# Hybrid attention and RG-LRU layer: column sums shared with TensorE, spread softplus chains, and fp32r for the F term and the gate sums

## The reference

```python
mod = silu(c) @ w_ada + b_ada                    # 4096 -> 3 x 4096
shift, scale, gate_res = split(mod, 3)
h = rms(x) * norm_w * (1 + scale) + shift
q, k, v, z_a, f_logit, x_r, z_r = split(h @ w_in)
log_f = log_sigmoid(f_logit + b_f)               # 16 heads
F = cumsum(log_f)
logit[t, s] = q_t . k_s / sqrt(128) + F_t - F_s  # s <= t
y_a = (softmax(logit) @ v * silu(z_a)) @ w_br_attn
xc = causal_depthwise_conv(x_r)                  # 4 taps
a = exp(-8 * sigmoid(xc @ w_rg_a + b) * softplus(-lru_lambda))
hr = scan(a, sqrt(1 - a*a) * sigmoid(xc @ w_rg_x + b) * xc)
y_r = (hr * silu(z_r)) @ w_br_rnn
g_a, g_r = split(sigmoid(h @ w_gate + b_gate))
x = x + gate_res * ((g_a * y_a + g_r * y_r) @ w_out)
```

## Time and profile before

| | |
|---|---|
| median of 3 runs | 2666.55 us (2666.18 to 2667.52) |
| the profiled execution: its time, its span | 2662.13 us, 2660.3 us |
| mean granted TensorE clock | 0.992 |
| TensorE busy | 2585.8 us, 97% of the span |
| VectorE busy | 1930.0 us, 73% |
| ScalarE busy | 1229.5 us, 46% |
| GpSimd busy | 1.2 us |
| DMA | 698.71 MB, mean 263 GB/s |

### The profile page before, as it was taken

One profiled execution on the slowest core, in us unless ns is written; L12 is line 12 of the kernel. 1 busy time (PEld: TensorE's weight loads), 2 busy tenths in 40 slices (PEclk: granted clock), 3 DMA queues, 4 the chain that ended last, 5 costly groups with the idle time before them and its releaser, 6 DMA issues.

```text
span 2660.3 us, 30834 instructions
## 1 busy us (share of the span) xinstructions
PE 2585.8 (97%) x11618; PEld 2134.1 (80%) x11618; DVE 1930.0 (73%) x1949; ACT 1229.5 (46%) x1428; POOL 1.2 (0%) x9
## 2 busy tenths in 40 slices
PE   2999999999999899999999999999999999999999
PEld 2788888888888788777888888878888888888887
DVE  6889999898887556666666666668787878745454
ACT  4554333333343356544656666654343433433333
POOL 0000000000000000000000000000000000000000
PEclk7999999999999999999999999999999999999999
DMA  9999999999998466444666666679898989667675
GB/s 370 327 335 345 330 353 337 338 355 335 348 338 279 128 193 186 120 127 145 196 199 195 199 191 200 197 252 353 306 355 305 353 305 356 216 208 225 209 225 171
DMA packets 351033, 698.71 MB, mean 263 GB/s; under 512 B 26306, under 2 KB 30628, under 8 KB 350628
## 3 DMA queue, kind: packets, MB, share of 16 engines
q1 hardware_dynamic: 350884, 696.74, 78.4%
HBM read 692.45 MB, written 4.19 MB: 262 GB/s over the span
## 4 chain that ended last, share of the span: by engine, by line
PE 93%; DVE 4%; DMA 1%; ACT 1%; issue 1%; SPq 0%; DVEq 0%; ACTq 0%
PE ps_acc L1027 30%; PE ps_acc L1029 30%; PE ps_acc L1036 30%; DVE acc L685 2%; DMA land<-in_w_gate 1%; PE ps_t L1087 1%; PE ps_t L1086 1%; ACT w_hi L510 1%; DVE w_lo L668 1%; PE ps_c L1054 1%; PE ps_t L1131 1%; DMA ada_first<-in_w_ada 0%; PE ps_t L1123 0%; DVE qn L837 0%; PE ps_t L1140 0%
## 5 line engine op out<-in xcount | busy, mean ns | idle before, releaser
L668 DVE TENSOR_TENSOR w_lo<-land,w_hi 128x1024 fp32r<-128x1024 f32 x896 | 1094.7, 1223 | 625.0 <-ACT w_hi L510 624.0
L510 ACT ACTIVATE w_hi<-land 128x1024 fp32r<-128x1024 f32 x896 | 950.5, 1061 | 1285.6 <-PE ps_acc L1029 1069.8
L1027 PE MATMUL ps_acc<-w_hi,h_hi 128*128 128x512 f32 x3072 | 1208.8, 393 | 6.4 <-issue 4.3
L1029 PE MATMUL ps_acc<-w_hi,h_lo 128*128 128x512 f32 x3072 | 1199.4, 390 | 0.0
L1036 PE MATMUL ps_acc<-w_lo,h_hi 128*128 128x512 f32 x3068 | 822.7, 390 | 8.2 <-DVE w_lo L668 8.2
L1036 PEld LDWEIGHTS ps_acc<-w_lo,h_hi 128*128 128x128 f32 x3068 | 576.6, 188 | 130.4 <-DVE w_lo L668 10.3
L1027 PEld LDWEIGHTS ps_acc<-w_hi,h_hi 128*128 128x128 f32 x3072 | 578.4, 188 | 127.2 <-issue 4.3
L1029 PEld LDWEIGHTS ps_acc<-w_hi,h_lo 128*128 128x128 f32 x3072 | 579.0, 188 | 118.3
L685 DVE SCALAR_TENSOR_TENSOR acc<-ada_ring,cvec,acc 128x1024 f32<-128x1024 f32 x217 | 277.7, 1280 | 3.8 <-DMA ada_ring<-in_w_ada 3.5
L926 DVE SCALAR_TENSOR_TENSOR racc<-res_land,cvec,racc 128x1024 f32<-128x1024 f32 x124 | 158.6, 1279 | 1.0 <-DMA res_land<-in_w_ada 1.0
L780 DVE TENSOR_TENSOR store<-ps_acc,store 128x1024 f32<-128x1024 f32 x89 | 108.6, 1220 | 11.8 <-PE ps_acc L1036 11.5
(11 more groups left out here) (168 smaller groups left out, 1027.4 us busy)
## 6 DMA issues: line engine op xcount, KB each, us to landing
land<-in_w_in SPq DMA_DIRECT2D x384, 512.0 KB, 4.9
land<-in_w_gate SPq DMA_DIRECT2D x256, 512.0 KB, 4.5
ada_ring<-in_w_ada SPq DMA_DIRECT2D x224, 512.0 KB, 5.9
res_land<-in_w_ada SPq DMA_DIRECT2D x128, 512.0 KB, 7.1
land<-in_w_out SPq DMA_DIRECT2D x128, 512.0 KB, 4.5
land<-in_w_br_attn SPq DMA_DIRECT2D x64, 512.0 KB, 4.2
land<-in_w_br_rnn SPq DMA_DIRECT2D x64, 512.0 KB, 5.3
ada_first<-in_w_ada SPq DMA_DIRECT2D x32, 512.0 KB, 11.5
```

The lines of the kernel that those rows point to most:

```text
L510: act.activation(w_hi[:, n % PARTS], land[:, n % LAND], ACT.Copy).then_inc(hi_rdy, 1)
L668: dve.tensor_tensor(w_lo[:, n % PARTS], land[:, n % LAND], w_hi[:, n % PARTS].bitcast(F32), ALU.subtract).then_inc(split_done, 1)
L1027: pe.matmul(ps_acc[:, par, t], l_hi(kk, t), w_hi[:, n % PARTS, kk], start=first and kk == 0, stop=False)
L1029: ins = pe.matmul(ps_acc[:, par, t], l_lo(kk, t), w_hi[:, n % PARTS, kk], start=False, stop=False)
```

## The change

- **First adaLN group.** Even tiles stay on VectorE (in slot 3 of `acc`), odd ones go to TensorE: eight fp32 products a tile, the tile as stationary operand and a column of silu(c) as moving one, added up in ps_c and ps_d (`first_tile`). Behind odd tiles 11 to 25 TensorE turns two pieces of x each. The last tile and the sums are made in two halves, and shift and scale, rounding and low parts follow in two halves. SyncE waits for a slot of an odd tile on a count of TensorE's.
- **Small loads** of parameters go from SyncE's queue to ScalarE's. `bf_col` is loaded once, not twice.
- **Softplus** of lru_lambda runs in the first stage, behind tile 24; its exp on ScalarE stands behind the last `take_xt`. The F chain is cut into nine steps between N_F + 7 and N_F + 20.
- **F_t - F_s** is one fp32r product of 64 rows: F split in a high and a low part, on both sides, put in place once by four DMAs; GpSimd multiplies the left side with a one-hot column for each head, into two buffers. `f_product` runs once, 16 columns wide.
- **Heads.** ScalarE instead of VectorE copies the turned probabilities; the maxima come negated from the reduction; on VectorE the head steps come ahead of `head_pre`. The value step waits for ya_lo of the head before, not of the one before that.
- **RG-LRU**: TensorE turns x_r and z_r straight from `store`, without the copy `xz`.
- **Gates**: racc is split in high and low parts and summed by four fp32r products; RES_AT is 5 + t*5//4 for 2 + t*4//3; the sums come four units later; the bias lands in `res_gate` itself; SyncE's wait for unit_done stands at N_R + 4.
- **Last unit**: all 12 products go by row blocks (six for t = 0, then six for t = 1), not only the last four.

```diff
+def ada_done(a):
+    return a // 2 + 1 if a < ADA_T else ADA_T // 2 + a - ADA_T + 1
...
+RSUM_AT = [N_R + (q + 1) * 2 * (GU + RU) for q in range(CH // 2)]
...
-        RES_AT[N_R + q * 2 * (GU + RU) + 2 + t * 4 // 3] = (q, t)
+        RES_AT[N_R + q * 2 * (GU + RU) + 5 + t * 5 // 4] = (q, t)
...
+            pool.wait_ge(f_rows, 64)
+            pool.wait_ge(f_cols, 1)
+            for h in range(HEADS):
+                if h >= 2:
+                    pool.wait_ge(scored, h - 1)
+                pool.tensor_scalar(f_head[:, h % 2], f_left[:], onehot[:, h:h + 1], None, ALU.mult
+                                   ).then_inc(fh_rdy, 1)
...
+                    if a >= FIRST_SLOTS and a % 2:
+                        sp_.wait_ge(ada_by_pe, (a - FIRST_SLOTS) // 2 + 1)
+                    elif a >= FIRST_SLOTS:
+                        sp_.wait_ge(ada_used, ada_done(a - FIRST_SLOTS))
...
+                if n == N_F + 23:
+                    sp_.wait_ge(f_ones, 2)
+                    sp_.wait_ge(f_low, 3)
+                    sp_.dma_start(f_left[32:48, :], f_hi[:].bitcast(F32)).then_inc(f_rows, 16)
+                    sp_.dma_start(f_left[48:64, :], f_rest[:, 0]).then_inc(f_rows, 16)
+                    sp_.dma_start(f_right_raw[0:16, :], f_rest[:, 2]).then_inc(f_rows, 16)
+                    sp_.dma_start(f_right_raw[16:32, :], f_rest[:, 1]).then_inc(f_rows, 16)
...
+                if n == N_R + 4:
+                    sp_.wait_ge(unit_done, N_R)
                 if n in RES_AT:
                     q, t = RES_AT[n]
                     i = q * RES_TILES + t
-                    if i == 0:
-                        sp_.wait_ge(unit_done, N_R)
...
+            act.wait_ge(sp_in, 1)
+            act.activation(spt[:, 1], spt[:, 0], ACT.Exp, scale=-1.0).then_inc(sp_e, 1)
             hi(0)
-            round_h(0)
+            round_first(0)
             hi(1)
+            round_first(1)
...
+                if step == "probs":
+                    act.wait_ge(pr_t, h + 1)
+                    if h:
+                        act.wait_ge(valued, h)
+                    act.activation(prt[:], ps_p, ACT.Copy).then_inc(prt_rdy, 1)
...
+                if n + 2 in RSUM_AT:
+                    q = RSUM_AT.index(n + 2)
+                    act.wait_ge(res_used, (q + 1) * RES_TILES)
+                    if q:
+                        act.wait_ge(rsum, q)
+                    act.activation(racc_hi[:], racc[:], ACT.Copy).then_inc(racc_h, 1)
...
-            for a in range(ADA_T):
+            for a in range(0, ADA_T, 2):
                 ada(a)
-                if a == 2:
+                if a == 4:
                     dve.wait_ge(ss_rdy, NT)
                     dve.tensor_scalar(mx[:], mx[:], 1.0 / D, EPS, ALU.mult, ALU.add).then_inc(ms_rdy, 1)
-                if a == 5:
                     dve.wait_ge(rt_rdy, 1)
                     dve.reciprocal(rstd[:], mx[:]).then_inc(rstd_rdy, 1)
-            mod_h(0)
-            low_h(0)
+                if a == 24:
+                    softplus()
+            mod_tiles(0, KPG // 2, 1, 0)
+            low_tiles(0, KPG // 2, 1)
+            mod_tiles(KPG // 2, KPG, 2, 1)
+            lo(0)
+            low_tiles(KPG // 2, KPG, 2)
...
+            def f_step(off):
+                part = lambda k: lt[:, k]
+                if off == 7:
+                    dve.wait_ge(bf_in, 16)
+                    dve.wait_ge(f_done, 1)
+                    st.did(dve.tensor_scalar(lt[:, 5], bank4[0:HEADS, 0:SEQ], bf_col[:], None, ALU.add))
                     st.sync()
-                    st.did(dve.memset(t_[ones_at:ones_at + 16, :], 1.0))
-                dve.wait_ge(bf_in, 32)
-                dve.wait_ge(f_done, 2)
-                st.did(dve.tensor_scalar(lt[:, 5], bank4[0:48, 0:SEQ], bf_col[0:48, 0:1], None, ALU.add))
-                st.sync()
-                st.did(dve.scalar_tensor_tensor(lt[:, 0], lt[:, 5], -1.0, lt[:, 5], ALU.mult, ALU.max), lf_in, 1)
-            def f_scan():
-                dve.wait_ge(lf_e, 1)
-                log1p_exp(lambda k: lt[:, k])
-                st.did(dve.tensor_scalar(lt[:, 5], lt[:, 5], 0.0, None, ALU.min))
-                st.sync()
-                st.did(dve.scalar_tensor_tensor(lt[:, 5], lt[:, 2], -2.0, lt[:, 5], ALU.mult, ALU.add))
-                st.did(dve.memset(lt[:, 4], 1.0))
-                st.sync()
-                st.did(dve.tensor_tensor_scan(ff[:], lt[:, 4], lt[:, 5], 0.0, ALU.mult, ALU.add))
-                st.sync()
+                    st.did(dve.scalar_tensor_tensor(lt[:, 0], lt[:, 5], -1.0, lt[:, 5], ALU.mult, ALU.max), lf_in, 1)
+                if off == 10:
+                    dve.wait_ge(lf_e, 1)
+                    log1p_ratio(part)
+                if off == 11:
+                    log1p_square(part)
+                if off == 12:
+                    log1p_terms(part, 6, 5)
+                if off == 13:
+                    log1p_terms(part, 4, 3)
+                if off == 14:
+                    log1p_terms(part, 2, 1)
+                if off == 15:
+                    log1p_end(part)
+                    st.did(dve.tensor_scalar(lt[:, 5], lt[:, 5], 0.0, None, ALU.min))
+                    st.sync()
+                    st.did(dve.scalar_tensor_tensor(lt[:, 5], lt[:, 2], -2.0, lt[:, 5], ALU.mult, ALU.add))
+                if off == 16:
+                    st.did(dve.memset(lt[:, 4], 1.0))
+                    st.sync()
+                    dve.tensor_tensor_scan(ff[:], lt[:, 4], lt[:, 5], 0.0, ALU.mult, ALU.add).then_inc(f_sum, 1)
+                if off == 20:
+                    dve.wait_ge(f_rnd, 1)
+                    dve.tensor_tensor(f_rest[:, 0], ff[:], f_hi[:].bitcast(F32), ALU.subtract).then_inc(f_low, 1)
+                    dve.tensor_tensor(f_rest[:, 1], f_hi[:].bitcast(F32), ff[:], ALU.subtract).then_inc(f_low, 1)
...
-                    dve.tensor_copy(prt[:], ps_p).then_inc(prt_rdy, 1)
...
+            def last_unit_by_rows(par, l_hi, l_lo, n):
+                for t in range(NT):
                     for kk in range(UK):
-                        for t in range(NT):
-                            ins = pe.matmul(ps_acc[:, par, t], l_hi(kk, t), w_lo[:, n % PARTS, kk],
-                                            start=False, stop=last and kk == UK - 1)
+                        pe.matmul(ps_acc[:, par, t], l_hi(kk, t), w_hi[:, n % PARTS, kk], start=False, stop=False)
+                        pe.matmul(ps_acc[:, par, t], l_lo(kk, t), w_hi[:, n % PARTS, kk], start=False, stop=False)
+                    if t == 0:
+                        pe.wait_ge(split_done, n + 1)
+                    for kk in range(UK):
+                        ins = pe.matmul(ps_acc[:, par, t], l_hi(kk, t), w_lo[:, n % PARTS, kk],
+                                        start=False, stop=kk == UK - 1)
...
+            def first_tile(a, kks):
+                pe.wait_ge(ada_first_in[a % FIRST_SLOTS], a // FIRST_SLOTS * 16 + 16)
+                for kk in kks:
+                    for s in range(2):
+                        ins = pe.matmul(first_bank(kk)[:, s * KPG + kk:s * KPG + kk + 1],
+                                        ada_first[:, a % FIRST_SLOTS, s, kk * P:(kk + 1) * P], cvec[:, a:a + 1],
+                                        start=a == 1 and s == 0 and kk % (KPG // 2) == 0, stop=False,
+                                        skip_group_check=True)
+                return ins
+            def first_sums(kks):
+                for kk in kks:
+                    for s in range(2):
+                        ins = pe.matmul(first_bank(kk)[:, s * KPG + kk:s * KPG + kk + 1],
+                                        acc[:, FIRST_ACC, s, kk * P:(kk + 1) * P], ones[:, 0:1], start=False, stop=True,
+                                        skip_group_check=True)
+                ins.then_inc(colsum, 1)
...
-                        pe.matmul(out, fl[:, t * P:(t + 1) * P], fr[:, 0:(t + 1) * P], start=True, stop=False)
+                        pe.matmul(out, f_head[:, h % 2, t * P:(t + 1) * P], f_right[:, 0:(t + 1) * P], start=True,
+                                  stop=False)
...
-                        pe.wait_ge(ya_rdy, h - 1)
+                        pe.wait_ge(ya_rdy, h)
...
+            pe.wait_ge(silu_c, 1)
+            for a in range(1, ADA_T - 1, 2):
+                first_tile(a, range(KPG)).then_inc(ada_by_pe, 1)
+                if 11 <= a < 27:
+                    for i in range(a - 11, a - 9):
+                        turn_x(i)
+            halves = range(KPG // 2), range(KPG // 2, KPG)
+            first_tile(ADA_T - 1, halves[0])
+            pe.wait_ge(ada_used, ada_done(ADA_T - 2))
+            first_sums(halves[0])
+            first_tile(ADA_T - 1, halves[1])
+            first_sums(halves[1])
...
+                    for i, bank in enumerate((ps_c, ps_d)):
+                        pe.matmul(bank[:], ones_r[:], racc_hi[:, i * CW:(i + 1) * CW], start=True, stop=False)
```

(63 more changed lines are left out.)

310 lines of the change are left out of this document (158 added, 152 removed).

## The result

The changed kernel takes 2649.57 us (median of 4 runs, 2649.00 to 2650.48), the kernel before 2666.36 us beside it (4 runs): ratio 0.9937 [0.992, 0.9954], faster by 16.8 us and by more than the 0.2% bound. Forecast were 2628 and a gain of 38: the sign holds and the time lies in the range, but less than half of the gain came.

The account below looks back on a forecast made before the run. TensorE's stream of 896 weight units bounds the kernel. Terms 2.5 + 10.9 + 9.9 + 6.7 + 1.8 + 2.1 + 3.2 + 1.3 = 38.4 us off 2662.1, plus 4.4, give 2628 us; range 2616 to 2653.

Parts of the forecast that it names:

- The step that failed: First adaLN group: back-to-back one-column products raise TensorE's clock too; the start was to gain 2.5 us.
- the second case: TensorE stays at 1.2 GHz through the first stage, unit 0 at 89 us: 2650 us, chance 0.24.
- the first: All terms as forecast, unit 0 near 67 us: 2628 us (own range 2617 to 2636), chance 0.58.
- The 0.8 us for a TensorE that has been busy: At unit 0: TensorE, busy before, pays only half of the low clock's price, another 0.8 us gained.
- F stage: 903 to 933 us: VectorE's softplus and F chain in one go make w_lo late; spreading gains 10.9 us, worst 8.
- F term: Score step of each head: two fp32r products take 0.43 us instead of 1.05, gaining 9.9 us over 16 heads.
- The waits for prt: Heads: VectorE's copy of turned probabilities holds TensorE up 10 times; copying on ScalarE gains 6.7 us.
- the 1.8 us of the forecast: Heads: the longest stall for the probability copy dropped the clock; with it short the clock holds, gaining 1.8 us.
- Gates, sums, tail: Gates: moved SyncE wait gains 2.1 us; racc sums as fp32r products 3.2; last unit by rows 1.3.
- the third: Stalls return in part, qkt behind the probability copy or VectorE's F steps beside evictions: 2638 us, chance 0.11.
- The fourth: TensorE's half of the first group eats all gains, needing 0.27 us a record; 2710 us at 0.43, chance 0.04.
- The fifth: F stage and heads lose as before for an unseen cause, only short terms remain: 2658 us, chance 0.03.

Follow-up runs that it names:

- experiment 3: Changed kernel with 120 needless identity transposes on TensorE ahead of the first tile, one-column products kept: 2649.78 us, one run.
- experiment 2: Changed kernel with operands exchanged in TensorE's first-group tiles, silu(c) column stationary and 512 tile columns moving, last tile and sums not halved: 2630.14 us.
- experiment 1: Changed kernel with all 32 tiles of the first adaLN group back on VectorE, TensorE making only transposes and sums: 2628.13 us.
- Experiments 4 and 5: Changed kernel with six first-group tiles on TensorE instead of sixteen: 2630.86 us; the same with softplus and its exp moved early: 2625.00 us.
- experiment 6: Changed kernel with the F chain on VectorE in one go at N_F + 14 instead of spread: 2655.30 us.
- experiment 7: Changed kernel with the F term of the scores as an fp32 product on the same 64 rows: 2656.48 us.
- the four kernels: Changed kernel with VectorE's head order new or old, and ScalarE or VectorE copying turned probabilities: 2649.57 (new, ScalarE), 2650.50 (new, VectorE), 2651.10 (old, ScalarE), 2655.24 us (old, VectorE).
- experiment 8: Changed kernel with VectorE again copying the turned probabilities, the new VectorE order kept: 2650.50 us.
- experiment 9: Changed kernel with head_pre ahead of the head steps on VectorE again, ScalarE's copy kept: 2651.10 us.

## Why the prediction was wrong

**The step that failed** is in the start: "I take it that one-column products, back to back, raise it too". Here they didn't. In the changed kernel 272 of them in 72 us stay at 0.213 apart, in experiment 3 the clock fell from 2.4 GHz among them and did not come back, and in experiment 2 it rose with the same tiles when 512 columns moved. That put the second case in the place of the first: unit 0 at 89.49 (second case: 89), 2649.57 us (2650). The sign of the evidence was there: the only one-column rows at the start ran at 0.50, and I set them aside as too short; the rise came in rows of 128 moving columns and I carried it over to a product of another shape. The second case deserved the larger chance.

**Luck in the second case.** Its mechanism and unit 0 are right, but that 2650 was met to half a microsecond is two errors that cancel. Behind unit 0 the change brought 32.4 us for 36.7 forecast; and the 4.4 us put on top, for a profiled execution of before below its median, did not recur: that of after was 0.9 above.

**The clock by the Trainium skill.** The Trainium skill, "TensorE: Matmul & The Clock Gate", section Part 4: PE-mode transpose, says that full speed does not engage in transposes. Experiment 3 disagrees: 15 us of transposes, and the half tile behind them takes 1.02 instead of 1.86. The same page of the Trainium skill, section Part 1: The HAM clock gate, says that the clock is set by how busy TensorE has been. Here the row of 60 to 90 us shows the engine busy for 28.97 of 30 us at the low pitch, so a high busy time as the profile counts it did not bring the high level.

**The rest of the start.** With the clock's part taken away (experiment 1) unit 0 comes at 67.97, 0.7 us before the old kernel. Experiments 4 and 5 show the late exp that I had costed: it holds VectorE 4.1 us, and moving it with softplus brings unit 0 5.9 us forward. The 0.8 us for a TensorE that has been busy failed with the same step: units 0 and 1 took 8.14 us for 7.53, and 7.3 to 8.4 in the experiments.

**F stage:** right in place and size (11.7 for 10.9), by the mechanism forecast for about half (experiment 6). Of the other 6 us 0.3 are the F product, and the rest goes with softplus by argument alone. The reading took all 48 missing products for waiting; 1.9 of the 10.9 us were the low clock behind the stall, as the granted 0.89 of that row could have told.

**F term:** right in mechanism, the size 7.1 for 9.9 (experiment 7). The pair takes 0.25 + 0.31 = 0.56 us, I took 0.43, and I counted the head at which TensorE waits anyway. The 256-column product costs 0.31 behind one of another operand, not the 0.117 of a row of like ones.

**The waits for prt:** 8.5 us forecast with the clock; what is left of the heads' 16.5 after experiment 7's 7.1 is 9.4. The cause was half right. With ScalarE's copy alone 1.6 us would be left, with the order alone 2.1. Both together are 5.8; the last 3.7 (9.4 - 5.8) I put down to the work that VectorE no longer has for fl, fr and the negation, which was argued and not tried. 2.4 of the 3.7 lie in the four waits that none of the four kernels has. The low clock behind a stall, the 1.8 us of the forecast, is seen again in experiment 8 (1.4 us).

**Gates, sums, tail:** right within 1 us. A racc sum is four products, the first at 1894.8 and the next unit at 1895.73:

```profile
L1301 PE MATMUL ps_c<-racc_hi,ones_r x4: 389/389/389, 1894.8 to 2297.3; 128*128 128x512 f32 x4
L1301 PE MATMUL ps_d<-racc_hi,ones_r x4: 389/389/389, 1895.3 to 2297.7; 128*128 128x512 f32 x4
...
1895.73 0.39 PE L1102 MATMUL ps_acc<-w_hi,h_hi 128*128 128x512 f32 x1
```

0.9 for 1.8 before, 3.4 us for four. About 1 us of it is given back at the wait at L1238 above; the kernels of all experiments show that wait too, and its cause was not tried. SyncE's wait gave 1.7 for 2.1; the same code took 65.28 us instead of 65.89 in all ten experiments, which would make it 2.3.

**The other cases:** the third did not come (no stall in the F stage, 0.6 us in the heads). The fourth, the slower side, needed 0.27 us a record; it was 0.213. The fifth fell with 32 us gained behind unit 0.

## What to carry over

Before idle TensorE time is filled, look at which operand moves: half a tile took 1.7 us at the low clock in either form here, and only the form with 512 moving columns got the high one. Work that is given to the engine that bounds the kernel must be priced at the clock of its own stretch, from rows of its own shape, and the branch for which only rows of another shape speak is not the likely one. Two edits that end the same wait don't add up; a table of two by two shows it.

## What the runs showed of the hardware

- Among one-column fp32 products TensorE's clock did not rise in the changed kernel: 0.213 us a record from 17 to 89 us with almost no gap, and with eight transposes between two tiles at eight places. In experiment 3 it was 2.4 GHz at their start and 1.2 GHz by the third half tile. Behind 120 transposes, and behind 16 (experiments 3 and 5), records ran at the high level, and with 512 moving columns they did from the third half tile on (experiment 2).
- The granted clock of the windows reads 1.00 from 60 to 90 us in the changed kernel, while its records stand 0.213 apart; for the same records in experiment 3 it reads 0.50. At the start of the changed kernel the pitch of the records is to be believed, not that column.
- Whether a stall in the stream lets the clock fall is not settled by its length: behind 1.04 us at the second head it fell (experiment 8, granted 0.66 from 1085 to 1090, unit 353 takes 4.30 us), behind 1.31 us at the same place it didn't (experiment 9, 1.00 and 2.93).
- An fp32r product of 64 rows between products of other operands takes 0.25 us with 128 moving columns and 0.31 with 256; in a row of like products 256 columns take 0.12.
